# Building part of the down projection's low weights with an accumulating DMA instead of a VectorE subtraction

## What is computed

```python
h = rms_norm(x, norm_mlp_pre[l])
u = jnp.square(jax.nn.relu(jnp.einsum('bsd,df->bsf', h, w_up[l])))      # 256 x 8192
x = x + rms_norm(jnp.einsum('bsf,fd->bsd', u, w_down[l]), norm_mlp_post[l])   # w_down: 8192 x 2048
```

## Time and profile before

| | |
|---|---|
| Runs | 1935.31, 1935.59, 1935.81 us; median 1935.59 |
| Span of the profiled execution, first to last instruction | 1933.5 us |
| Own time of the profiled execution | not listed apart; the runs are 1.8 to 2.3 us above its span |
| TensorE (PE) busy | 1922.0 us, 99% |
| Weight loads (PEld) | 1601.5 us, 83% |
| VectorE (DVE) | 1250.8 us, 65% |
| ScalarE (ACT) | 983.0 us, 51% |
| GpSimd (POOL) | 17.8 us, 1% |
| DMA | 415.48 MB, mean 215 GB/s |

### The profile page before, as it was taken

One profiled execution on the slowest core, in us unless ns is written; L12 is line 12 of the kernel. 1 busy time (PEld: TensorE's weight loads), 2 busy tenths in 40 slices (PEclk: granted clock), 3 DMA queues, 4 the chain that ended last, 5 costly groups with the idle time before them and its releaser, 6 DMA issues.

```text
span 1933.5 us, 21919 instructions
## 1 busy us (share of the span) xinstructions
PE 1922.0 (99%) x8770; PEld 1601.5 (83%) x8770; DVE 1250.8 (65%) x1255; ACT 983.0 (51%) x951; POOL 17.8 (1%) x31
## 2 busy tenths in 40 slices
PE   9999999999999999999999999999999999999998
PEld 7888888888888888888888888888889888888886
DVE  7747658845666644445466666677587869676655
ACT  6334445646445444444455555555555546544543
POOL 0000000000000000000000000000000000000000
PEclk9999999999999999999999999999999999999999
DMA  9876977765777388888886555565687544556753
GB/s 323 251 231 174 267 257 216 233 246 196 241 228 255 112 241 246 239 240 243 244 248 204 192 191 189 193 231 181 188 222 253 185 164 156 176 174 224 231 203 109
DMA packets 386151, 415.48 MB, mean 215 GB/s; under 512 B 192509, under 2 KB 205057, under 8 KB 385409
## 3 DMA queue, kind: packets, MB, share of 16 engines
q1 hardware_dynamic: 385032, 412.49, 68.6%
q10 hardware_dynamic: 1016, 1.59, 0.2%
HBM read 388.86 MB, written 25.17 MB: 214 GB/s over the span
## 4 chain that ended last, share of the span: by engine, by line
PE 95%; DVE 2%; ACT 1%; issue 1%; POOL 0%; POOLq 0%; DVEq 0%; ACTq 0%
PE acc L1589 92%; PE mis L1589 3%; ACT hi L578 1%; DVE lo L994 1%; DVE m L976 1%; PE mis L1592 1%; ACT m L567 0%; DVE m L984 0%; DVE at L1036 0%; ACT at L617 0%; DVE m L1294 0%; ACT xs L567 0%; DVE xs L976 0%; DVE sm L984 0%; POOLq L1892 0%
## 5 line engine op out<-in xcount | busy, mean ns | idle before, releaser
L1589 PE MATMUL acc<-hi,at 128*128 128x512 f32 (+1 forms) x5344 | 1650.6, 388 | 0.3 <-DVE lo L994 0.3
L1589 PEld LDWEIGHTS acc<-hi,at 128*128 128x128 f32 x5344 | 1000.4, 188 | 201.7 <-DVE lo L994 1.2
L994 DVE TENSOR_TENSOR lo<-raw,hi 128x2048 fp32r<-128x2048 f32 (+1 forms) x333 | 752.9, 2264 | 529.6 <-ACT hi L578 529.3
L1589 PE MATMUL acc<-lo,at 128*128 128x512 f32 (+1 forms) x2672 | 1032.5, 387 | 0.0
L578 ACT ACTIVATE hi<-raw 128x2048 fp32r<-128x2048 f32 (+1 forms) x333 | 628.4, 1891 | 522.0 <-PE acc L1589 476.7
L1589 PEld LDWEIGHTS acc<-lo,at 128*128 128x128 f32 x2672 | 501.8, 188 | 98.6
L567 ACT ACTIVATE m<-acc,st 128x512 f32<-128x512 f32 (+2 forms) x104 | 69.6, 669 | 86.3 <-PE acc L1589 85.2
L976 DVE TENSOR_TENSOR m<-m 128x256 f32<-128x256 f32 (+1 forms) x145 | 75.1, 518 | 20.9 <-ACT m L567 16.4
L567 ACT ACTIVATE m<-m 128x512 f32<-128x512 f32 (+4 forms) x71 | 58.2, 819 | 53.2 <-DVE m L976 37.9
L1043 DVE TENSOR_TENSOR at<-m,at 128x1024 fp32r<-128x1024 f32 x64 | 78.0, 1219 | 2.8 <-ACT at L628 2.8
L628 ACT ACTIVATE at<-m 128x1024 fp32r<-128x1024 f32 x64 | 66.6, 1041 | 7.5 <-PE acc L1589 7.5
(11 more groups left out here) (134 smaller groups left out, 529.9 us busy)
## 6 DMA issues: line engine op xcount, KB each, us to landing
raw<-in_w_in SPq DMA_DIRECT2D x133, 1024.0 KB, 5.3
raw<-in_w_up SPq DMA_DIRECT2D x64, 1024.0 KB, 6.4
raw<-in_w_down SPq DMA_DIRECT2D x64, 1024.0 KB, 5.1
raw<-in_w_out SPq DMA_DIRECT2D x32, 1024.0 KB, 5.2
m<-turned SPq DMA_DIRECT2D x144, 128.0 KB, 4.6
raw<-in_w_pg SPq DMA_DIRECT2D x16, 1024.0 KB, 5.2
turned<-m SPq DMA_DIRECT2D x28, 512.0 KB, 6.0
raw<-in_w_in SPq DMA_DIRECT2D x12, 688.0 KB, 5.1
```

The lines of the kernel that those rows point to most:

```text
L994: e.tensor_tensor(lo, raw, hi.bitcast(F32), ALU.subtract).then_inc(s_lo.on("lo", n))
L1589: return e.matmul(o, a, b, start=start, stop=stop)
```

## The change

For fourteen chunks of the down projection, 177, 181, and so on to 229, `lo` is made in another way. ScalarE, having written `hi`, writes a second rounded copy with the sign turned into `lo` (the raw chunk times -1). Then GpSimd issues a DMA that reads the same chunk of `w_down` from HBM once more and adds it to `lo` in SBUF, which gives `raw - hi`. VectorE leaves these chunks out. TensorE waits for the rounding and for the DMA. SyncE's next load into the raw buffer waits for the negated copy. The count of matmuls and all other chunks are as before.

```diff
+BY_DMA = tuple(range(N_DN + 1, N_DN + 56, 4))
...
             def raw(n):
                 if nth[n] >= NRAW:
-                    sp.wait_ge(s_lo, "lo", order[nth[n] - NRAW])
+                    last = order[nth[n] - NRAW]
+                    sp.wait_ge(*((s_neg, "neg", last) if last in BY_DMA else (s_lo, "lo", last)))
...
             for n in range(N_ALL):
+                if n + LEAD in BY_DMA:
+                    c = n + LEAD
+                    po.wait_ge(s_neg, "neg", c)
+                    e.dma_start(lo_of(c).rearrange("p (k c) -> p k c", c=512), chunks[c][0], accum_op=ALU.add).then_inc(
+                        s_add.on("added", c), 16)
...
                 e.activation(hi_of(n), raw_of(n), ACT.Copy).then_inc(s_hi.on("hi", n))
+                if n in BY_DMA:
+                    e.activation(lo_of(n), raw_of(n), ACT.Copy, scale=-1.0).then_inc(s_neg.on("neg", n))
...
             def low(n):
+                if n in BY_DMA:
+                    return
...
-                if n > 2:
+                if n in BY_DMA:
+                    pe.wait_ge(s_hi, "hi", n)
+                    pe.wait_ge(s_add, "added", n)
+                elif n > 2:
                     pe.wait_ge(s_lo, "lo", n)
```

More of the change, by code:

```diff
@@ L109, in program @@
         s_lo = Count(sem("s_weights_lo"))
+        s_neg = Count(sem("s_weights_neg"))
+        s_add = Count(sem("s_weights_added"), 16)
         s_ach = Count(sem("s_act_high"))
@@ L116, in program @@
         s_out2 = Count(sem("s_out_act"), 16)
-        counts = [s_prod, s_pe, s_hi, s_lo, s_ach, s_act, s_dve, s_pool, s_out, s_out2, *s_raw]
+        counts = [s_prod, s_pe, s_hi, s_lo, s_neg, s_add, s_ach, s_act, s_dve, s_pool, s_out, s_out2, *s_raw]
         s_ld = {}
```

## The result

The changed kernel takes **2036.11 us** (median of four runs, 2033.94 to 2038.39), the kernel before 1935.45 us beside it (1935.20 to 1935.81): a ratio of 1.0519, 95% interval 1.0507 to 1.0531. That is 100.7 us more. The profiled execution took 2038.39 us with a span of 2036.6, so 103.1 us over the span of before.

What follows compares the result with a forecast made beforehand. PE was taken as the bound, so relieving VectorE gains nothing; fourteen late adds of 5.0 us each, 70 us, on the profiled span of 1933.5 us plus about 2.1 us around it gave 2006 us, range 1949 to 2075.

Steps and rivals of the forecast that it cites:

- What bounds the kernel: Whole kernel: PE, busy 99% of the span, is the bound; removing 32 us of VectorE's subtractions gains nothing.
- ScalarE's negation, SyncE's load, GpSimd's queue: Changed chunks: negation of 1.82 us fits the 5.44 us period, load starts 0.5 us earlier, GpSimd's issue is under 2 us.
- the sum: Whole kernel: 14 x 5.0 = 70 us of lateness on the kernel before, 2006 us, 3.6% slower.
- The lateness: PE's wait at each changed chunk for the add's landing: 5.0 us, taken between 4.6 and 6.4.
- The double cost: GpSimd's add on the DMA engines: two reads for each write, 6.2 us of work, landing 11.3 us after issue.
- the upper bound: PE's wait at a changed chunk: 6.4 us late, as the load of chunk 185 shares the engines with the add's end.
- its own bounds: Time of the changed kernel for 4.0 to 6.4 us of lateness per changed chunk: 1992 to 2025 us.
- the wider range: Time of the changed kernel, 1949 to 2075 us, leaving out cases that fit or gain and most of the slowest.
- the clock falls as well: PE after each stall: half granted clock adds 2.2 us to 5.0, 101 us in all, 2036 us; chance 0.22.
- the wrong case: Stalls at the changed chunks: double cost of the add with the clock staying full, 2006 us; chance 0.36.
- The other side: PE's wait at chunk 181: the add lands within 6.7 us of the negation, time stays 1936 us; chance 0.10.

Runs made afterwards that it cites:

- plain_copy: The changed kernel with GpSimd's DMA copying the chunk over the negated weights instead of adding it (products differ): 1953.09 us, ratio 1.0092 to the kernel before.
- warm_wait: The changed kernel with 20 idle matmuls of 256 columns ahead of PE's wait for each add: 2027.06 us, ratio 1.0456 to the kernel before.

## Why the prediction was right, and where it was not

- **What bounds the kernel**: right. PE's waits and its clock are the whole loss, and relieving VectorE is worth nothing even when the add is hidden (ratio 1.0007, 0.9997 to 1.0016).
- **ScalarE's negation, SyncE's load, GpSimd's queue at nothing by themselves**: right for the first (1.0001). The load that starts beside the add costs by contention, as the sum had it. GpSimd's queue is not free: the issue takes 1.28 us, 0.54 longer for an add than for a copy, and that is time to the landing.
- **The lateness**, 5.0 us between 4.6 and 6.4: PE stood idle for 5.07 us on average. That the number is so close is in part luck, as its parts were off in opposite directions. The double cost is confirmed (206 GB/s against 416). But a copy is 1.0 us late and not 1.5 (it lands 7.5 us after its issue, where I had 8.2), and the add then lands 4.6 us after the copy (12.1 against 7.5), where I had 3.1 for the second read. Of the 4.6, alone on the engines adding costs 3.0 (8.4 against 5.4): 0.54 of longer issue, which I had put at nothing, and 2.5 of second read. The 1.6 that are left fit the next load, which is issued 5.7 us behind the add and shares the engines with its end, as the upper bound said; no run takes this load out by itself.
- **The sum**, 2006 us: this step failed. It held the fourteen waits and took the granted clock as unchanged, and the measured 2036.1 us lie outside its own bounds, 1992 to 2025; the wider range, 1949 to 2075, holds them because it takes in the rivals. The rival "the clock falls as well" came true, near the price worked out for it: 2036 us forecast, with 2.2 us for each stall, where the clock took 2.0. In numbers: all fourteen groups of matmuls behind a stall are slower than the 22.04 us that they take without a fall, by 1.3 to 2.8 us, 27.8 us in all (57.39 us in place of 22.04 for the longer last group). With 71.0 us of waits and 14 x 0.27 us, by which 22.04 exceeds the 21.77 of an unbroken stream, that makes 102.6 of the 103.1 us.
- **Why the wrong case was chosen as the likelier**: from one place, the end of the kernel, I read that the clock falls 3.8 us after PE's last work, took this for a length that a gap has to reach, and held against the rival that the shorter lateness of 4 us leaves under 4 us idle. But the sum itself had stalls of 5.0 us, longer than the 3.8, so the row spoke for the rival at the very lateness that was forecast. The other ground, that PE is busy without a gap before each stall, did not help either: with gaps of 4.0 to 5.7 us the clock fell fourteen times of fourteen, each behind more than 20 us of unbroken work. Nor is 3.8 us a length that a gap has to reach: the runs show falls after gaps of 1.85 and 2.94 us, and none after others of 2.97 and 3.46.
- **The other side**, that the add fits into 6.7 us: it is what the copy alone does (5.4), and what no add of a whole chunk did: 8.4 from HBM and 7.0 from SBUF, even with the engines to itself.
- **Rules of the Trainium skill**: "Collectives: The Full Stack", section "The bandwidth ceiling", has the second source read halve the rate. The trace agrees for rows of 2 KB from HBM, 206 against 416 GB/s; the 254 GB/s with 8 KB rows within SBUF have no copy of the same form beside them. By the fit in "DMA: Bandwidth & Descriptors", section "Anatomy of one DMA — SWDGE (gpsimd) path", the estimate for 1 MB is 4.4 us; measured are 5.4 for a copy alone, 7.5 beside a load, and 8.4 to 12.1 for an add from HBM. Here the measurements decide.

What stays open is which gaps of under 4 us make the clock fall: they went both ways, and no run settles it. Those of 4.0 us and more in these runs all did.

## What to carry to other kernels

Before work moves from an engine that waits to a DMA, compare the whole latency of the DMA, at the moment at which it would be issued and with the transfers already issued there, with the slack that the consumer leaves; busy shares say nothing about this, as 44% of idle DMA time in the stage didn't help. A stall of the matmul engine can cost more than its length: here 5.07 us of waiting cost 7.2. A wait of 4 us or more that recurs should be priced with the clock at half speed behind it, and a shorter one, of 2 to 3.5 us, as a chance of it. What is late can be asked for last: reordering the 24 matmuls of a changed chunk regained 75 us of the 101, and moving one load out of the way all but 1 us of the rest.

## What the runs showed of the hardware that I had not expected

- The granted clock fell to 0.50 behind a gap of only 1.85 us, in one of fourteen stalls of that run (`plain_copy`), and held through one of 3.46 us in another (`warm_wait`). In the change it came back 4.7 us after PE had started again at 1061.99, and about 4.0 us after the start at 1120.85; the price was 1.3 to 2.8 us for each stall.
- The issue on GpSimd took 0.74 us for a copy of 1 MB, 1.28 us for an add with 2 KB rows, 0.87 us for an add with 8 KB rows, and 1.20 us for an add of half the bytes in 2 KB rows: nearly as long as for all of them.
- An add within SBUF with 8 KB rows landed 1.0 us sooner than with 2 KB rows (7.0 against 8.0 us), at 254 against 191 GB/s.
